# Thirty-two experts streamed through SBUF: fifteen weight slots in place of twelve, with TensorE's small steps put in another order

## The reference

```python
def expert_block(args):
    e, x_b = args
    gu = x_b @ w_gu[e] + b_gu[e]
    gate = jnp.minimum(gu[..., ::2], SWIGLU_LIMIT)
    up = jnp.clip(gu[..., 1::2], -SWIGLU_LIMIT, SWIGLU_LIMIT)
    return ((up + 1.0) * (gate * jax.nn.sigmoid(SWIGLU_ALPHA * gate))) @ w_dn[e] + b_dn[e]
...
y = jnp.zeros((T + 1, D), yb.dtype).at[slot_tok].add(yb * slot_g[:, None])[:T]
```

## Time and profile before

| | |
|---|---|
| median of 3 runs (lowest, highest) | 2769.97 us (2766.5, 2770.57) |
| the profiled execution, its own time | 2768.43 us |
| its span, first to last instruction | 2766.6 us |
| TensorE busy in the span | 96% |
| mean granted TensorE clock | 0.988 of full |
| moved by DMA | 637.28 MB, 230 GB/s over the span |

### The profile page before, as it was taken

The page is one execution under the profiler, slowest core; times in us unless marked ns, Lnnn a source line. Parts: engine busy times, 40 slices in busy tenths (PEclk is TensorE's granted clock), DMA queues, the critical chain, the costliest instruction groups (busy, mean ns, idle before and its releaser), DMA issues.

```text
span 2766.6 us, 41104 instructions
## 1 busy us (share of the span) xinstructions
PE 2645.6 (96%) x17543; PEld 1706.4 (62%) x17543; DVE 734.3 (27%) x1593; ACT 442.8 (16%) x854; POOL 11.5 (0%) x24
## 2 busy tenths in 40 slices
PE   9999999999999999999998998799999999999997
PEld 7777887777768877788788887333333334333332
DVE  1003600010017200134655555322212221221213
ACT  0001400010013200224422214111111110111111
POOL 0000000000000000000000000000000000000000
PEclk9999999999999999999999999899999999999999
DMA  8445244444443444552200104699989999999985
GB/s 292 171 152 201 96 182 153 153 187 152 153 191 128 167 152 152 198 194 94 79 18 3 48 3 142 280 421 421 421 339 421 421 421 375 391 420 421 421 355 225
DMA packets 88292, 637.28 MB, mean 230 GB/s; under 512 B 10264, under 2 KB 10264, under 8 KB 11504
## 3 DMA queue, kind: packets, MB, share of 16 engines
q1 hardware_dynamic: 86400, 628.62, 57.5%
q0 software_dynamic: 1744, 6.43, 1.0%
HBM read 632.38 MB, written 2.62 MB: 230 GB/s over the span
## 4 chain that ended last, share of the span: by engine, by line
PE 56%; issue 40%; DVE 3%; ACT 1%; DMA 0%; DVEq 0%; POOLq 0%; POOL 0%; SPq 0%
PE ps L621 22%; PE ps L632 11%; PE ps L828 6%; PE ps L719 4%; PE ps L779 2%; PE ps L1082 1%; PE ps L1079 1%; PE ps L1069 1%; DVE arena L2120 1%; PE ps L691 1%; PE ps L599 1%; PE ps L985 1%; PE ps L864 1%; PE ps L875 1%; DVE arena L2083 0%
## 5 line engine op out<-in xcount | busy, mean ns | idle before, releaser
L621 PE MATMUL ps<-X,ring 128*128 128x256 f32 x2816 | 617.3, 380 | 7.1 <-DMA ring<-weights 6.5
L621 PEld LDWEIGHTS ps<-X,ring 128*128 128x128 f32 x2816 | 535.6, 190 | 96.2 <-issue 25.4
L1246 PE MATMUL ps<-ring,arena 128*64 128x512 f32 (+1 forms) x1536 | 380.5, 599 | 1.2 <-DMA ring<-weights 1.2
L1246 PE MATMUL ps<-arena 128*64 128x512 f32 (+1 forms) x1536 | 372.4, 592 | 0.0
L632 PE MATMUL ps<-ring,arena 128*128 128x512 f32 x704 | 308.6, 592 | 0.0
L1246 PEld LDWEIGHTS ps<-ring,arena 128*64 128x64 f32 (+1 forms) x1536 | 130.1, 144 | 217.8 <-issue 208.9
L1246 PEld LDWEIGHTS ps<-arena 128*64 128x64 f32 (+1 forms) x1536 | 126.5, 142 | 219.1 <-issue 215.8
L1763 DVE TENSOR_TENSOR arena<-ps,arena 128x512 f32<-128x512 f32 x44 | 30.4, 691 | 819.7 <-PE ps L621 812.3
L632 PEld LDWEIGHTS ps<-ring,arena 128*128 128x128 f32 x704 | 133.8, 190 | 151.3 <-issue 149.2
L828 PE MATMUL ps<-arena,ring 128*128 128x256 f32 x784 | 173.0, 380 | 0.0
L828 PEld LDWEIGHTS ps<-arena,ring 128*128 128x128 f32 x784 | 147.7, 190 | 25.0 <-issue 5.6
(11 more groups left out here) (469 smaller groups left out, 2323.9 us busy)
## 6 DMA issues: line engine op xcount, KB each, us to landing
ring<-weights SPq DMA_DIRECT2D x402, 1024.0 KB, 8.0
arena<-weights SPq DMA_DIRECT2D x192, 1024.0 KB, 13.4
con<-consts SPq DMA_DIRECT2D x1, 1872.5 KB, 13.6
vec<-vectors SPq DMA_DIRECT2D x1, 1671.5 KB, 16.4
rel_scratch<-arena POOLq DMA_DIRECT2D x1, 1536.0 KB, 38.1
arena<-moe_bias POOLq DMA_DIRECT2D x1, 1152.0 KB, 12.1
X<-x_t SPq DMA_DIRECT2D x2, 512.0 KB, 5.4
ring<-weights SPq DMA_DIRECT2D x2, 512.0 KB, 6.5
```

What stands on the lines that cost most here:

```text
L621: last = mm(dst[:, f, :], w[:, k, f * P:(f + 1) * P], X[:, k, :], start=(k == 0), stop=(k == KD - 1))
L1246: last = mm(put(half), stationary(4 * kq + k), SLOTS[j][:, k * 512:(k + 1) * 512], start=False, stop=(kq == 1 and k == 3))
```

## The change

There are fifteen slots, and the blocks go round them: block g goes to slot g mod 15 and is loaded once block g-15 has been used. Two of the new slots are parts of `con` and `vec`, the tables of constants and vectors, whose entries are laid out anew so that what the experts still need lies outside; the third is half in `vec` and half in `con` and is filled by two loads of 512 KB. Blocks 12, 13 and 14 are now loaded ahead of pass 0. `combine` is split into its token halves: n = 1 stays behind the gate product, n = 0 comes behind `gather`; for this `PTE` is held twice. The bias of the down product no longer waits for ACT's copy. In a wide pass both halves stay, the transposes of step 3 move into the middle of the second product (the change's title says gate product: it is one half of gate and up), and `across` comes ahead of the transposes of `AC`. Ahead of a wide pass ACT copies the transposed activation first and the gathered tokens after it. Some semaphores are folded into shared ones.

```diff
+SLOT_COUNT = 15
 ADA0 = LAYERS * LAYER_BLOCKS
...
-        SLOTS = [ring[:, (MOE_AT + j) % RING, :] for j in range(RING)] + [area(a, BLK)[0] for a in (8192, 10240, 12288, 26260, 28308, 15932)]
+        con_slot, split = CON["cos"][0], CON["level_b"][0]
+        assert CON["level_b"][0] - con_slot == BLK and NCON - split >= BLK // 2 and VEC["b_router"][0] + EXPERTS >= 3 * BLK // 2 <= VEC["w_router"][0]
+        SLOTS = ([(ring[:, (MOE_AT + j) % RING, :],) for j in range(RING)]
+                 + [(area(a, BLK)[0],) for a in (8192, 10240, 12288, 26260, 28308, 15932)]
+                 + [(con[:, con_slot:con_slot + BLK],), (vec[:, 0:BLK],), (vec[:, BLK:3 * BLK // 2], con[:, split:split + BLK // 2])])
+        assert len(SLOTS) == SLOT_COUNT and GROUP * EXPERT_BLOCKS % SLOT_COUNT == 0
...
+
+        def loaded_by(E, i, j, lap, extra):
+            g = EXPERTS * EXPERT_BLOCKS + j if extra else block_at(E, i, j)
+            s = g % SLOT_COUNT
+            each = 16 * len(SLOTS[s])
+            done = each * (g // SLOT_COUNT + 1) + (16 * MOE_BEFORE[s] if s < RING else 0)
+            if extra:
+                return s, E * each + (done - EXPERTS * each)
+            if isinstance(E, int):
+                return s, done
+            return s, lap * (each * (GROUP * EXPERT_BLOCKS // SLOT_COUNT)) + done
 
         CTX_TILES, X_TILES = tiles(CTX_BLOCKS, CTX_AT), tiles(X_BLOCKS, X_AT)
...
-            def expert(E):
-                who = sp.value_load(WHO[0:1, bass.ds(E, 1)], min_val=0, max_val=EXPERTS - 1)
-                for j in range(EXPERT_BLOCKS):
-                    sp.wait_ge(block_used, E * EXPERT_BLOCKS + (MOE_AT + j + 1 - EXPERT_BLOCKS))
-                    expert_block(who, j)
+            def expert_block(who, j, s):
+                at = 0
+                for part in SLOTS[s]:
+                    n = part.shape[1]
+                    sp.dma_start(part, weights[who * EXPERT_BLOCKS + (MOE0 + j), :, at:at + n]).then_inc(slot_of(s), 16)
+                    at += n
+
+            def chosen(E):
+                return sp.value_load(WHO[0:1, bass.ds(E, 1)], min_val=0, max_val=EXPERTS - 1)
 
             ordered(RING, OUT_AT + 2)
...
-            expert_block(0, 6)
+            expert_block(0, 6, 6)
+            expert_block(1, 0, 12)
             ordered(OUT_AT + 2, MOE_AT + 2)
             sp.wait_ge(b3_ready, 1)
...
             sp.wait_ge(mg_half, 2)
-            expert_block(0, 11)
+            expert_block(0, 11, 11)
             for j in range(2, RING):
                 sp.wait_ge(block_used, MOE_AT + j - RING + 1)
-                expert_block(0, j)
+                expert_block(0, j, j)
             sp.wait_ge(f_tok, 2)
             for j in range(7, 9):
-                expert_block(0, j)
-            for j in range(EXPERT_BLOCKS):
-                sp.wait_ge(block_used, MOE_AT + j + 1)
-                expert_block(1, j)
+                expert_block(0, j, j)
+            sp.wait_ge(mask_ready, 2)
+            sp.wait_ge(pe_step, PE_STEP["pos_done"])
+            expert_block(1, 2, 14)
+            for j in range(3, EXPERT_BLOCKS):
+                g = EXPERT_BLOCKS + j
+                sp.wait_ge(block_used, MOE_AT + g - SLOT_COUNT + 1)
+                expert_block(1, j, g % SLOT_COUNT)
             sp.wait_ge(extra_ready, 1)
-            with sp.Fori(FIRST, EXPERTS) as E:
-                expert(E)
+            with sp.Fori(0, WIDES) as K:
+                for i in range(GROUP):
+                    who = chosen(K * GROUP + (FIRST + i))
+                    for j in range(EXPERT_BLOCKS):
+                        g = (FIRST + i) * EXPERT_BLOCKS + j
+                        sp.wait_ge(block_used, K * (GROUP * EXPERT_BLOCKS) + (MOE_AT + g - SLOT_COUNT + 1))
+                        expert_block(who, j, g % SLOT_COUNT)
             extra = sp.value_load(FLAG[0:1, 0:1], min_val=0, max_val=EXTRA - 1)
             with sp.If(extra > 0):
                 with sp.Fori(EXPERTS, extra + EXPERTS) as E:
...
-                def combine(E, i, wide):
+                def combine(E, i, wide, n):
+                    kept = PTES[(i - 1) % 2]
                     pe.wait_ge(yb_ready, E + i)
-                    for n in range(2):
-                        for half in range(2):
-                            rows = slice(0, P) if wide else two(half)
-                            yb = YBE[rows, half * 512:(half + 1) * 512] if wide else YBE[rows, 0:512]
-                            last = mm(ps[:, (6, 2)[n] + half, :], PTE[rows, n, :], yb, start=True, stop=True)
-                        last.then_inc(comb_done, 1)
+                    if n == 0 and not (isinstance(E, int) and E + i < 2):
+                        pe.wait_ge(comb_read, E * 2 + (2 * i - 2))
+                    for half in range(2):
+                        rows = slice(0, P) if wide else two(half)
+                        yb = YBE[rows, half * 512:(half + 1) * 512] if wide else YBE[rows, 0:512]
+                        last = mm(ps[:, (6, 2)[n] + half, :], kept[rows, n, :], yb, start=True, stop=True)
+                    last.then_inc(comb_done, 1)
...
+                    late = not (first or wide or extra)
...
                             mm(put(half), chooser[0:96, 0:P if wide else CAP], B3[0:96, c:c + 512], start=True, stop=False)
+                        if biased:
+                            biased()
...
                     products(0, token, SELG, 0, 0)
+                    def slots_across():
+                        if wide:
+                            pe.wait_ge(comb_read, E * 2 + 2 * i)
+                        for n in range(2):
+                            last = nc.tensor.transpose(ps[:, 6 if wide else 4, n * P:(n + 1) * P], ON[:, n, :], ident)
+                        last.then_inc(pt_turned, 1)
+
                     if first:
                         turns_across()
                     else:
-                        combine(E, i, after)
-                        if wide:
-                            pe.wait_ge(comb_read, E * 2 + (2 * i - 1))
-                    for n in range(2):
-                        last = nc.tensor.transpose(ps[:, 6 if wide else 4, n * P:(n + 1) * P], ON[:, n, :], ident)
-                    last.then_inc(pt_turned, 1)
-                    products(4 if wide else 1, token, SELG, 1024, 4, turns_placed if first else None)
+                        combine(E, i, after, 1)
+                        if not late:
+                            combine(E, i, after, 0)
+                    if not wide:
+                        slots_across()
+                    products(4 if wide else 1, token, SELG, 1024, 4, turns_placed if first else slots_across if wide else None)
                     if not first:
-                        pe.wait_ge(comb_read, E * 2 + 2 * i)
+                        pe.wait_ge(comb_read, E * 2 + (2 * i - 1))
                     gather(E, i + 1, ahead)
+                    if late:
+                        combine(E, i, after, 0)
+                    if wide:
+                        across(E, i + 1, ahead)
                     pe.wait_ge(glu_done, E * 2 + (2 * i + 3))
                     pe.wait_ge(pte_ready, E + (i + 1))
                     for q in range(8 if wide else 4):
                         last = nc.tensor.transpose(ps[:, (6 if wide else 4) + q // 4, (q % 4) * P:(q % 4 + 1) * P], AC[:, q * P:(q + 1) * P], ident)
                     last.then_inc(act_turned, 1)
-                    across(E, i + 1, ahead)
-                    pe.wait_ge(actt_ready, E + (i + 1))
-                    pe.wait_ge(seld_ready, E + (i + 1))
+                    if not wide:
+                        across(E, i + 1, ahead)
+
+                    def turned():
+                        pe.wait_ge(actt_ready, E + (i + 1))
 
                     def hidden(k):
...
-                    products(4 if wide else 5, hidden, SELD, 2048, 8)
+                    pe.wait_ge(seld_ready, E + (i + 1))
...
                     n = 512 if wide else 256
+                    kept = PTES[1 if extra else i % 2]
                     for c in range(2):
                         act.wait_ge(clipped, E * 2 + (2 * i + c + 1))
                         act.wait_ge(glu_done, E * 2 + (2 * i + c + 1))
                         A(SGM[:, 0:n], TG[:, 0:n], ACT.Sigmoid, scale=1.702).then_inc(sigm_ready, 1)
                         if c == 0:
                             act.wait_ge(pt_turned, E + (i + 1))
-                            A(PTE[:, :, :].rearrange("p n s -> p (n s)"), ps[:, 6 if wide else 4, 0:2 * P], ACT.Copy).then_inc(pte_ready, 1)
-                    tokens(E, i + 1, ahead)
+                            A(kept[:, :, :].rearrange("p n s -> p (n s)"), ps[:, 6 if wide else 4, 0:2 * P], ACT.Copy).then_inc(pte_ready, 1)
+                    if not ahead:
+                        tokens(E, i + 1, ahead)
                     act.wait_ge(act_turned, E + (i + 1))
                     if wide:
```

(8 more changed lines are left out.)

130 lines of the change are left out of this document (70 added, 60 removed).

## The result

The changed kernel takes 2738.11 us (median of 4 runs, 2735.35 to 2740.26), the kernel before 2769.44 us (2766.5 to 2770.57) beside it: a ratio of 0.9889, 95% interval 0.9872 to 0.9906, 31 us faster. In another job it took 2737.89 us, ratio 0.9901 (0.9880 to 0.9921). The forecast was 2728 us with a range of 2721 to 2737: right in sign and in most of the mechanism, 10 us too low, and the measurement lies 1.1 us outside the range. The profiled execution took 2738.19 us, with a span of 2736.4.

The account below looks back on a forecast made before the run. Both TensorE and the stream of weights were taken to matter, weights deciding when pass 28 starts: 35.2 us gained there, 6.4 behind it, less 1.5 for pairs, is 40.1 us from 2768.43: 2728 us, range 2721 to 2737.

Parts of the forecast that it names:

- excess of the wide passes: Wide passes took 56.83, 55.50 and 53.80 us; the excess over 53.80, 3.0 + 1.7 = 4.7 us, was counted as gained.
- anchor of part 2: Weights alone: from block 96's landing at 1981.4, less 7.5 us, 2.491 us a block, so block 331 lands at 2559.3.
- Split: Half a combination fills the 0.64 us wait between gather and transposes in 25 narrow passes: 16.0 us gained.
- Bias: Bias matmuls of the second product moved ahead of the wait for ACT's copy: 0.24 us in 26 narrow passes, 6.2 us.
- Wide waits: In each wide pass, the 2.87 us wait and parts of two smaller ones go: 3.8 us each, 11.4 in all.
- part 1: TensorE alone, as if weights were never late: 41.8 us gained in all; pass 28 would start at 2571.2.
- Late weights: Waits for weights just ahead of the wide passes, in passes 7, 17 and 27: 3.8 us (2.3 + 2 x 0.75).
- Rival 1: The weights bind less or not at all: gain up to 45.6 us, 2723 us; chance 0.13.
- Rival 2: Slower wide passes, with waits for weights in passes 17 and 27 just ahead: 2731 to 2734 us; chance 0.18.
- Rival 3: The slots work but the filled gaps in narrow passes don't: gain 23.4 us, 2745 us; chance 0.08.
- rival 4: The change does nothing that counts, as the stream of weights is at its rate before too; chance 0.03.
- rival 5: Halves that pay a load's fixed part, 4.4 us more for each of 21 pairs: 2819 us; chance 0.05.

Follow-up runs that it names:

- fifteen_old_order: Changed kernel with its fifteen slots but the old order of the other engines, DVE's additions in wide passes excepted: 2768.37 us, ratio 0.9996 to the kernel before.
- no_wide: Changed kernel with the wide passes' transposes again ahead of their gate product and the crossing behind the activation's transposes: 2754.03 us, ratio 0.9948.
- sp_unrolled_before: Kernel before, twelve slots, with only SyncE's loop written out for ten passes instead of one: 2767.46 us, ratio 1.0001.
- short-loop version: Changed kernel with SyncE's loop rolled up to one lap of fifteen blocks, the next block read from a table: 2735.34 us, ratio 0.9880.
- no_split: Changed kernel with the combination in one piece again at the end of the pass: 2746.06 us, ratio 0.9910.

## Why the prediction was right and wrong

**Right.** All three mechanisms worked as it put them: no wait for the activation in narrow passes, no wait for DVE's additions in wide ones, no dip in the stream, waits for weights just ahead of wide passes 18 and 28 and hardly any behind 28. The weights and not TensorE decide when pass 28 starts. The excess of the wide passes over 53.80 us (4.7 us), which it tied to the idling ahead of the product, was gained in full; in fifteen_old_order and no_wide a longer wait brings it back, in each wide pass. That all 4.7 us were there to gain was luck: with the same wait of 2.87 us, sp_unrolled_before has none of it.

**The step that failed** is the anchor of part 2: "If it never idles, block g lands at 1981.4 - 7.5 + 2.491 (g - 96)." The stream never idled, and block 331 landed at 2568.8, 9.5 us late. Of these, 2.0 us were there at block 96. Its load:

```profile
L542 SPq DMA_DIRECT2D arena<-weights x1: 1088/1088/1088, 1951.8 to 1951.8; - x1
...
DMA to landing us min/median/max: 24.1/24.1/24.1
```

1951.8 + 24.1 = 1975.9, for 1973.9. The other 7.5 us came on the 235 blocks behind it: 592.9 us, 2.523 each and not 2.491. I had divided a block by a rate of 421 GB/s, read from stretches that look smooth, and took a full queue for a constant rate. Between gaps it is one: the median spacing is 2.487 us. But the gaps were there in the kernel before: its blocks 15 to 96, over which the stream never idled, landed in 203.5 us (1777.97 to 1981.45), 2.512 each, with three gaps of 0.6 to 0.9 us. At that rate block 331 comes 4.9 us later, about half of the miss. In the short-loop version block 331 landed at 2564.9, 3.9 us sooner, and the seven gaps right behind 8 KB packets add up to 4.7 us in the changed kernel, so about 4 us of the 9.5 hang on SyncE's written-out loop (theory A), which stands in the diff and which I had priced at nothing: the prediction counts the loads of every queue, and not the instructions that have to be fetched for them. The 5.6 us that remain there over the anchor are 1.0 at block 96 and 4.6 behind it, where seven irregular gaps of 0.3 to 1.1 us in its landings make up 4.7 us. Most of its gaps end 2 to 4 us behind a 16 KB packet of the other instruction queue, which has 36 or 37 packets in 1776:2690 in every version; but two thirds of those packets have no gap behind them. That they are the cause was not tried.

**Sizes.** At the start of pass 28 the prediction had 16.0 us from block 331's landing, and it is 16.9: the wait of 1.2 us for ACT did not go, but fell to 0.43. Behind it, it had 6.4 us of gain and 5.4 came: the last wide pass gave 3.25 (53.81 to 50.56) for 3.8, passes 29 and 30 gave 0.85 and 0.68 for 0.88, and pass 31 with the tail 0.64. So the shortfall is 9.5 + 0.9 + 1.0, less the 1.5 us allowed for pairs: 9.9 us, and 40.1 - 9.9 = 30.2 is what the profiled executions show (2768.43 to 2738.19).

*Split*: 0.64 x 25 = 16.0 forecast. It gave 0.50 a pass (27.36 in no_split, 26.86 with it), 12.5, in part because two halves cost 2.12 us where the whole cost 1.92. *Bias*: 0.24 forecast, 0.19 measured. *Wide waits*: 3.8 forecast, 3.25 measured, as 0.76, 0.31 and 0.76 us are left. Up to pass 28 none of these sizes mattered, since the weights were later. TensorE alone is found by taking the late weights off the changed kernel's start of pass 28: 1.1, 0.6, 3.8, 1.0 and 4.0 us in passes 7, 16, 17, 26 and 27 (over 26.86 in a narrow pass, 28.8 in one ahead of a wide one) are 10.5, 2585.7 - 10.5 = 2575.2. Less 3.0 of slow pass 0, and with the 1.9 us by which pass 0 began sooner than before (1758.56 for 1760.45), that is 2574.1 for 2571.2. So part 1 was 3 us too high up to there, and this little only by luck: passes 12 and 22 gave 2.3 each for 0.88. *Late weights* were read as 3.8 us (2.3 + 2 x 0.75); by the lengths of passes 7, 17 and 27, 29.33 each where weights are in time, they were 2.6, 1.0 and 1.2, 4.8 us.

**The rivals.** Rival 1, that the weights bind less, was the wrong side: they bind by 10 us, not 4. Rival 2 had the waits ahead of the wide passes right and their consequence wrong: pass 28 took 50.56 like the others. Rival 3 is refuted by the wait for the activation, gone from narrow passes, rival 4 by the 31 us, and rival 5, pairs that pay a fixed part, by a pair's 0.06 to 0.10 us. The range ended at 2737 since no case had a slower stream; the 2.512 us a block of the kernel before, gaps included, belonged in it.

**Open.** Adding SyncE fetches costs 0.7 us each; taking 14 away between blocks 15 and 331 gave back only 3.1 us (798.5 to 795.4). The landings say where the difference lies: in the changed kernel no gap follows the eleven packets ahead of the landing of block 210 (in its second profile one follows the last two of them), and one follows each of the seven from there on. Why the first ones cost nothing, these runs don't show. The version with the short loop has 2 us more of the other gaps behind block 96 (4.7 for 2.7), and what makes those is open too.

## What to carry to other kernels

When a stream of loads decides, price it by its landings over hundreds of blocks and not by the rate in its best stretch: 0.03 us a block, over 235 blocks, was a quarter of the whole gain here. Then what delays the stream counts in full (an instruction program that is fetched again in every lap, up to 0.7 us for each 8 KB), and what the compute engines lose ahead of their wait for it counts little, as long as the buffers don't fill up. Buffers and order are worth little apart and much together (0 to 5, 11 and 31 us), and with both made, where the long passes stand is worth some 5 us either way.

## What the runs showed of the hardware

- SyncE's instruction fetches show among the DMA packets, 8 KB each; their number follows its loop (4 short, 19 written out, 42 with eight more instructions a block). With the weights' queue always full each added fetch put all later landings back by 0.7 us (20 fetches, 14.3 us), while its own packet has 8 KB of the 1 MB of a block.
- A wait of 4.07 us on TensorE was followed by a lower granted clock in every wide pass in which it stood (0.83 over 2000:2010, products 0.9 to 2.5 us slower); waits of 2.87 us were followed by it in two of three passes of the kernel before, and in none of three in sp_unrolled_before.
- A load of 1 MB as two of 512 KB costs 0.06 to 0.10 us more in a full queue (2.55 us from landing to landing for 2.486; 4.1 to 4.3 us for 42 pairs).
- The rate of a full queue is constant only between gaps: a block of 1 MB every 2.487 us (median), 2.51 to 2.54 over stretches of 81 to 235 blocks.
